# Two sums of squares moved in TensorE's order: the gated norm of the first stage, and the residual after attention

## What is computed

```
y = y.reshape(b, l, SSD_WIDTH) * silu(z)
y = y.reshape(b, l, SSD_GROUPS, SSD_WIDTH // SSD_GROUPS)        # 2 groups of 512
y = y * rsqrt(mean(y * y, axis=-1, keepdims=True) + NORM_EPS)
out_b = y.reshape(b, l, SSD_WIDTH) * ssd_norm
mixed = concatenate([out_a, out_b], axis=-1)
x = x + mixed @ w_out                       # 2048 x 1024
x = x + swiglu(rmsnorm(x, ffn_norm))        # the next layer wants mean(x * x)
```

## Time and profile before

| quantity | value |
|---|---|
| median of three runs | 2073.42 us (2066.02 to 2075.84) |
| span of the profiled execution | 2070.8 us |
| PE busy | 1960.2 us, 95% |
| DVE busy | 1314.5 us, 63% |
| ACT busy | 704.8 us, 34% |
| mean granted TensorE clock | 0.980 of full speed |

### The profile page before, as it was taken

The page is one execution under the profiler, slowest core; times in us unless marked ns, Lnnn a source line. Parts: engine busy times, 40 slices in busy tenths (PEclk is TensorE's granted clock), DMA queues, the critical chain, the costliest instruction groups (busy, mean ns, idle before and its releaser), DMA issues.

```text
span 2070.8 us, 41540 instructions
## 1 busy us (share of the span) xinstructions
PE 1960.2 (95%) x18039; PEld 1806.4 (87%) x18039; DVE 1314.5 (63%) x1710; ACT 704.8 (34%) x1011; POOL 77.0 (4%) x123
## 2 busy tenths in 40 slices
PE   8998999999799999999998999898999998999898
PEld 8887999998599999989877889897988887889887
DVE  8895388747647866854765358566764576339555
ACT  5562233434623332130423132233231334122233
POOL 2000000000400000020000000000001000000000
PEclk9999999999999999999999999999999999999989
DMA  8544377853437794636430246354654540235433
GB/s 220 141 126 153 120 249 258 269 139 112 121 120 258 241 260 101 171 95 170 115 93 14 76 115 179 82 153 113 174 143 115 140 123 4 63 103 172 113 107 108
DMA packets 473063, 291.41 MB, mean 141 GB/s; under 512 B 26679, under 2 KB 467484, under 8 KB 472776
## 3 DMA queue, kind: packets, MB, share of 16 engines
q1 hardware_dynamic: 466688, 262.20, 45.1%
q0 software_dynamic: 5312, 25.32, 3.2%
q10 hardware_dynamic: 904, 1.58, 0.3%
HBM read 288.02 MB, written 1.05 MB: 140 GB/s over the span
## 4 chain that ended last, share of the span: by engine, by line
PE 82%; DVE 12%; ACT 3%; issue 2%; DMA 1%; POOL 0%; DVEq 0%; ACTq 0%; SPq 0%
PE bank L702 40%; PE bank L1412 6%; PE bank L1414 6%; PE bank L1413 6%; PE bank L691 4%; PE bank L661 2%; PE bank L891 2%; DVE rounded L727 2%; PE bank L883 2%; PE bank L784 1%; PE bank L1599 1%; PE bank L1612 1%; PE bank L1057 1%; PE bank L1580 1%; PE bank L1464 1%
## 5 line engine op out<-in xcount | busy, mean ns | idle before, releaser
L702 PE MATMUL bank<-rounded 128*128 128x256 f32 (+1 forms) x4440 | 540.7, 283 | 10.0 <-DVE rounded L727 7.5
L702 PEld LDWEIGHTS bank<-rounded 128*128 128x128 f32 (+1 forms) x4440 | 531.0, 189 | 16.5 <-DVE rounded L727 10.1
L727 DVE TENSOR_TENSOR rounded<-arena,rounded 128x1024 fp32r<-128x1024 f32 (+1 forms) x243 | 293.2, 1213 | 87.2 <-ACT rounded L716 69.1
L1412 PE MATMUL bank<-parts 128*128 128x256 f32 x1024 | 290.5, 284 | 2.4 <-DVE parts L2164 2.4
L1413 PE MATMUL bank<-parts 128*128 128x256 f32 x1024 | 289.8, 283 | 0.0
L1414 PE MATMUL bank<-parts 128*128 128x256 f32 x1024 | 289.7, 283 | 0.0
L702 PE MATMUL bank<-common,arena 128*128 128x256 f32 x1280 | 285.2, 380 | 0.0
L702 PEld LDWEIGHTS bank<-common,arena 128*128 128x128 f32 x1280 | 240.1, 189 | 39.6 <-issue 4.8
L767 ACT ACTIVATE arena<-bank 128x512 f32<-128x512 f32 x114 | 67.8, 598 | 440.5 <-PE bank L702 427.9
L1412 PEld LDWEIGHTS bank<-parts 128*128 128x128 f32 x1024 | 196.5, 192 | 3.2 <-DVE parts L2164 2.1
L1413 PEld LDWEIGHTS bank<-parts 128*128 128x128 f32 x1024 | 196.5, 192 | 0.1
(11 more groups left out here) (389 smaller groups left out, 2509.3 us busy)
## 6 DMA issues: line engine op xcount, KB each, us to landing
arena<-in_w_in SPq DMA_DIRECT2D x190, 512.0 KB, 3.8
whole<-in_ffn_w_gate_up SPq DMA_DIRECT2D x44, 1024.0 KB, 5.2
arena<-in_ada_w POOLq DMA_DIRECT2D x32, 768.0 KB, 6.5
whole<-in_ffn_w_down SPq DMA_DIRECT2D x16, 1408.0 KB, 7.2
arena<-in_rec_w_in SPq DMA_DIRECT2D x36, 512.0 KB, 3.8
arena<-in_att_w_qkv SPq DMA_DIRECT2D x24, 512.0 KB, 3.7
arena<-in_rec_w_out SPq DMA_DIRECT2D x16, 512.0 KB, 3.5
arena<-in_mla_w_o SPq DMA_DIRECT2D x16, 512.0 KB, 3.7
```

What stands on the lines that cost most here:

```text
L702: last = pe.matmul(psum[s][0:c, m % 2 * T:m % 2 * T + T], w[a][:, k, cols], x[b][:, k, :], start=(k, a, b) == (0, 0, 0), stop=k == job.kt ...
L727: dve.tensor_tensor(raw_view(job_of[u], u, UNIT_LOW), raw, high_view(job_of[u], u).bitcast(F32), ALU.subtract)\
L1412: pe.matmul(bank, w_hi, x_hi, start=start and k == 0, stop=False)
```

## The change

In `rec_pe` the second group's sum (`sums_pe(UU[:, 4:8], ...)`) moves from behind the units 6 and 7 of `rec_oa` to ahead of them. In `out_but_last_squares_pe` the places of the three sums become an argument. The recurrent layer keeps 2, 4 and 6; attention's output takes 3, 5 and 7.

```diff
-        def out_but_last_squares_pe(job, sq, pieces=None, begun=False):
+        def out_but_last_squares_pe(job, sq, pieces=None, begun=False, summed_at=(2, 4, 6)):
...
             def sum_before_last(i):
-                if i in (2, 4, 6):
-                    sum_pair_pe(bank, sq, i - 2, DK)
+                if i in summed_at:
+                    sum_pair_pe(bank, sq, 2 * summed_at.index(i), DK)
...
             sums_pe(UU[:, 0:4], 4, ready=act_squares)
+            sums_pe(UU[:, 4:8], 4, ready=act_squares)
             multiply_units(rec_oa, range(6, 8))
-            sums_pe(UU[:, 4:8], 4, ready=act_squares)
             pe.wait_ge(normed.sem, normed.due(pe))
             return out_but_last_squares_pe(rec_ob, H)
...
-            return out_but_last_squares_pe(att_out, H, begun=True)
+            return out_but_last_squares_pe(att_out, H, begun=True, summed_at=(3, 5, 7))
```

## The result

The changed kernel took 2062.18 us (median of 7 runs, 2057.56 to 2069.68) against 2073.42 us (median of 7, 2066.02 to 2080.3): a ratio of 0.9943 with a 95% interval of 0.9925 to 0.9961. 11.2 us are gone, and the interval stands for 8 to 16 us; the forecast was 11.0, and 2062.4 us. The span of the profiled execution is 2060.4 us against 2070.8.

What follows compares the result with a forecast made beforehand. PE was taken to bound the kernel, busy 95% of the span with 82% of the chain; 4.58 + 2.27 + 2.33 + 1.79 = 10.97 us off the median gave 2062.4 us, range 2055 to 2070 us.

Steps and rivals of the forecast that it cites:

- The waits: PE's idle time goes: 4.58 us behind the gated norm (L821), 2.33 us behind attention's square (L840).
- The slack: At the recurrent output, `normed` comes 2.3 us before PE needs it, at 196.06 against 198.38.
- The clock: Slow products behind both idle stretches go: 2.27 us at the recurrent output, 1.79 at attention's end; bounds from 0.
- The rival in which only the idle time goes: Both places: only 4.58 + 2.33 = 6.91 us go, the slow clock stays or turns up elsewhere; 2066.5 us, chance 0.25.
- 6.85 and 4.12: Wait plus clock by place: 4.58 + 2.27 us at the recurrent output, 2.33 + 1.79 at attention's end.
- the slower rival: Later code meets other clock moments; three more slow stretches eat 10.2 us, four give 2076.0 us; chance 0.06.
- the 10.4 us that count as faster: Whole program: about 0.5%, what a measurement can tell from no change; faster by over that got 0.49.
- The working of the chances: Forecast 0.55, about 0.44 of it over 10.4 us; idle time only 0.25, one part 0.14, clock's loss 0.06.
- six slow stretches: In the clock's loss case, only six or seven more stretches make the kernel over 0.5% slower; that got 0.03.
- What was late next: Behind both places nothing new waits: 1.7 us to spare for the addition to X, 2.9 for the low part.

Runs made afterwards that it cites:

- the filler kernel: The kernel before with 20 useless products in PE's wait for the gated norm and 10 ahead of attention's first sum of squares; 2071.38 us, ratio 0.9986.
- att_only: The kernel before with only attention's output sums one unit later, the gated norm's sums as before; 2068.86 us, ratio 0.9973.
- first_sum_only: The changed kernel with attention's output sums after units 3, 4 and 6 instead of 3, 5 and 7; one execution, 2062.65 us.

## Why the prediction was right

**The waits.** Both were priced at PE's idle time, 4.58 and 2.33 us, and both went, each alone and together. The slack was right to a tenth: between the norm's end and PE's need 2.3 us were forecast, 195.74 against 198.1 is what came, and the kernel with the sum between the units turned that slack into the 1.13 us of waiting that the same arithmetic gives.

**The clock.** The 2.27 and 1.79 us were argued from two stretches of one trace, with 0 as the other end. The fillers show that they were the price of the idle time: 2.25 and 1.69 us. They are not the same in each execution: in att_only it was 1.68 us behind the same 4.58 us. The Trainium skill, in "TensorE: Matmul & The Clock Gate", Part 1: The HAM clock gate, says as much of slow matmuls from run to run, and these two traces agree. The rival in which only the idle time goes (2066.5 us) is out at the two places: the filler kernel loses none of its waiting and its two distances are 3.94 us shorter all the same. For the whole program 2066.5 us would be a ratio of 0.9967, just above the changed kernel's interval.

**A small term that was missing.** The distances shrank by 7.10 and 4.28 us instead of 6.85 and 4.12. The filler kernel separates the parts: without the clock's 2.25 and 1.69 us, 4.85 and 2.59 us are left for waits of 4.58 and 2.33, so a stop costs 0.27 and 0.26 us beyond its length; in the kernel with the sum in between, 1.13 us of waiting cost 1.40, again 0.27. Some 0.17 us of it is overlap that the stop takes away: two units take 7.07 us and yet the next item starts 6.90 us after their start. The rest stays open. At attention the working had 0.10 us of this in its clock term, 1.79 against 1.69: the first sum behind the filled wait takes 0.97 us to the next unit at full clock, not 0.87.

**Given back on the way.** The SwiGLU product of the recurrent stage was forecast at 228.5 and came at 227.99; that behind attention was forecast at 579.7 and came at 580.58. The shift of 7.36 us at the first had become 563.21 - 557.44 = 5.77 us at the entry to the second place. Of the 7.36 us, 1.6 were given back, and the clock accounts for them. Before, then after, the windows of the same work:

```profile
445.00:475.00 30.00, 30.00 (x233) 29.04 (x232) 14.09 (x13) 8.25 (x10) 0.00 (x0) 0.94 0.48 140
545.00:562.00 17.00, 13.54 (x78) 9.75 (x75) 5.56 (x16) 7.93 (x21) 6.95 (x10) 0.90 0.00 1
```

```profile
438.00:468.00 30.00, 30.00 (x217) 30.00 (x216) 12.30 (x12) 7.56 (x9) 0.00 (x0) 0.83 0.40 118
538.00:556.00 18.00, 13.53 (x90) 9.56 (x88) 7.92 (x23) 10.08 (x28) 9.12 (x13) 1.00 0.02 5
```

Before, 0.06 x 30 + 0.10 x 17 = 3.5 us of full-speed time were withheld, after 0.17 x 30 = 5.1: 1.6 more. In the windows from 438 and 445 us PE never idled by its busy time. This is what the slower rival supposes, a later stretch that meets the clock otherwise, at 1.6 us here, about a sixth of the 10.2 us that it puts against the gain. That the earlier start brought it on is not shown: from 436 to 482 us the granted clock was 0.89 in att_only too, which came there only 0.8 us earlier than the kernel before, 0.93 in first_sum_only and 0.96 before.

**The size against the bound.** The forecast of 11.0 us lay just over the 10.4 us that count as faster; 0.57% came, with an interval of 0.39% to 0.75% that has 0.5% inside it. That the medians differ by 11.2 us, 0.2 from the forecast, is closer than such an interval can vouch for and in part luck: the two distances gave 11.38 us, 1.6 were given back between them, and the profiled spans differ by 10.4. The working of the chances has two slips. With a spread of 4 us either way and the bound 0.6 us below the forecast, an even spread puts (4 + 0.6) / 8 = 0.58 of the 0.55 above it, 0.32 and not 0.44. And six slow stretches cost 20.4 us, a net 9.4, which is not yet over 0.5%.

**What was late next.** Nothing, as forecast. Behind the gated norm DVE was through with its two `up_low_v` 1.75 us before the next addition to X, where 1.7 were forecast. The last low part at the end of attention ended at 582.26, 2.9 us ahead of the quarter that wants it, and `up_low_v` and the weights never appear among PE's waits of the two distances.

## What to carry to other kernels

When an engine idles for a result whose inputs were ready long before, look at what stands ahead of the producer's last input in a fixed order. Moving that input ahead of independent work cost nothing here, and it takes the wait away as long as the work behind it is longer than the chain: one unit of 3.45 us did not cover a chain of 4.6 us, two did.

Measure an edit by a distance between two fixed instructions inside one trace, not by the end of the program: where the clock stayed full, the first distance was 40.39 or 40.40 us in five kernels and the second 23.13 or 23.14 in six, while the runs of one kernel lie over 10 us apart.

## What the runs showed of the hardware

TensorE's idle time can cost more than its length. 4.58 us of it cost 2.25 or 1.68 us of slower products behind it, 2.33 us cost 1.69, 2.35 us cost 1.68, and 1.13 us cost no clock. Behind one and the same wait of 2.7 us the clock fell in five of ten traces. Products whose result nobody reads, 128 columns wide, kept the granted clock at 1.00 through the waits of 4.58 and 2.33 us. I had expected the loss to grow with the stall; in these executions 2.35 us cost as much as 4.58 did in another.

The clock also falls where TensorE is busy throughout by the profile, as in the windows from 438 and 445 us. In both stretches stand 48 products of one column (L1464). Before, they took 5.42 us, from 454.79 on, and the fall came right behind them; after, it began among them, and they took 8.33 us. What brings it down there was not tested.
